# Mixture-of-experts step: experts scattered in pairs, the first overflow job begun in the last turn of the loop

## The chip, the cores and the metric

The kernel runs on one core of one Trainium2 chip. The metric is the device time of one execution in microseconds (us), less is better. The engines are named as in the profile: PE is TensorE, PEld its weight loads, DVE VectorE, ACT ScalarE, POOL GpSimd, SP SyncE, which issues the weight loads from HBM.

## What is computed

One decoder layer in float32 on 320 tokens (256 of a prompt, 64 of samples), width 1024: a convolution and latent-attention mixer, attention into a memory, a layer of 32 experts of which each token takes four, and a final norm. The change touches the experts alone:

```
top_val, top_idx = top_k(h @ w_router + b_router, 4);  gates = softmax(top_val)
for each expert e and its tokens:
    g = min(x @ w_gate[e] + b_gate[e], 7);  u = clip(x @ w_up[e] + b_up[e], -7, 7)
    a = (u + 1) * (g * sigmoid(1.702 * g))
    y[token] += gate * (a @ w_down[e] + b_down[e])
```

Three matrices of 1024 x 1024 float32 belong to an expert, 12.58 MB, and all 32 experts are computed.

## The kernel before

The weights stream through `ring`, four slots of one matrix each, in halves of 2.1 MB: eight halves stand in it, six are used in a turn. SP issues the load of a half as soon as the product that used its place has ended (`refill`, L980), so a half is asked for eight halves ahead of its use, and every load of the expert loop and of the job behind it goes through this one queue in order.

An expert takes at most 64 tokens (`CAP`). The tokens beyond that go to overflow jobs, each of which is one more pass with the same expert's weights; the list `jobs` is computed on the chip. With the inputs here there is one job. Its loads follow those of the loop on SP at once.

A turn of the loop (L830 and on, eight rounds of four turns, so written that `q` is the expert's number modulo 4) runs on PE in this hand-written order:

- `biases` (L809), then the gate product (16 matmuls: two halves of the weights, four chunks, two halves of the output columns, of 64 stationary columns each) into bank 0;
- `scatter(0, ...)`: two matmuls (L822) that put the products of the expert before back onto the tokens 0 to 127, once for each half of the output columns. The stationary operand has 64 rows (the places of one expert) and 128 columns (tokens), so two of them lie in the array side by side in row halves. Results go to banks 6 and 7;
- the up product into bank 1;
- `gather` (L791): six matmuls that select the tokens of the next expert with a one-hot matrix `Ph`;
- `scatter(1, ...)`, tokens 128 to 255;
- `turn_gates` (three transposes of `Pg`, the one-hot matrix times gate), `turn(4, AA)` and `turn(3, XG)` (four transposes each, L319), then `scatter(2, ...)`, tokens 256 to 319;
- the down product into bank 2.

Beside it DVE makes the one-hots of the next expert (`one_hots_at`, L1660 to L1662), clips and multiplies (L1691 to L1702), adds each scattered half into `X` (`add_scattered`, L1674, six additions a turn) and moves the transposed tiles (L1706, L1666). ACT takes the sigmoid (L1254) and copies bank 2 to `XG` (L1257), bank 5 to `PgT` (L1260) and the down product to `Y` (L1263), where the lower 64 rows hold one half of the output columns and the upper 64 the other. `Y` and `PgT` have two buffers.

After the last turn PE scatters the last expert; DVE adds, raises `moe_idle`, and all engines read the number of jobs. Within a job the order is serial: DVE reads the expert's number, shifts the ranks and builds the one-hots (L1721, L1660), PE gathers (L791), turns the gates, ACT copies, PE turns the tokens, DVE moves them, then biases, gate, up, turn, down, scatter into banks 6/7, 0/1 and 3/4, and three wide additions (L1743). The final norm and the stores follow (L1280, L1753, L912).

## Time and profile before

| | us |
|---|---|
| median of three runs (1534.43, 1537.01, 1538.79) | 1537.01 |
| the profiled execution | 1537.16 |
| its span in the profile | 1535.3 |
| one turn of the expert loop | 29.64 |
| last down product of the loop ends | 1471.7 |
| down product of the job ends | 1520.4 |

The first 520 us are the mixer, the memory attention and the router. The expert loop runs from about 520 to 1472 us; the job and the final norm take the rest. The span is the time from the first to the last instruction shown; the execution's own time is 1.9 us longer. A time of an instruction is that of one profiled execution.

### The profile page before, as it was taken

To read this page: it belongs to the slowest core of one execution; us is meant where nothing else is said; L and a number is where in the kernel's file an instruction comes from. 1 tells how busy PE (TensorE), PEld (TensorE's weight loads), DVE (VectorE), ACT (ScalarE), POOL (GpSimd) and SP (SyncE) were. 2 spreads that over 40 slices of the span, in tenths; PEclk is the share of its full clock that TensorE was granted. 3 is DMA by queue.
4 is the path that set the end of the run, shared out by engine and by line. 5 is a ranking of instruction groups with operands and counts; after the bars stand their busy time and mean duration, and the time that the engine had idled before them with its cause. 6 is when DMAs were issued, how large, how long until landed. Compare 5 with 4: busy or idle time off the path is not lost.

```text
span 1535.3 us, 16367 instructions
## 1 busy us (share of the span) xinstructions
PE 1392.9 (91%) x6359; PEld 562.2 (37%) x6359; DVE 520.3 (34%) x1244; ACT 201.2 (13%) x409; POOL 15.9 (1%) x20
## 2 busy tenths in 40 slices
PE   7998667688775899999999999999999999999986
PEld 3574444344534233333333333333333333333322
DVE  1137976312324333223233233323323333232332
ACT  2123212301212000100100100010010010010001
POOL 0100011000000000000000000000000000000000
PEclk9999588899996799999999999999999999999978
DMA  9501011364044299999999999999999999999931
GB/s 341 206 10 36 1 62 62 141 244 194 0 168 175 101 405 422 426 426 423 423 422 429 422 426 426 423 425 425 426 422 426 426 420 426 426 423 421 426 130 35
DMA packets 44235, 463.40 MB, mean 302 GB/s; under 512 B 5174, under 2 KB 6134, under 8 KB 17828
## 3 DMA queue, kind: packets, MB, share of 16 engines
q1 hardware_dynamic: 42668, 453.54, 71.1%
q0 software_dynamic: 1536, 9.44, 1.7%
q8 instruction: 20, 0.33, 0.1%
q14 instruction: 11, 0.09, 0.0%
HBM read 460.04 MB, written 3.28 MB: 302 GB/s over the span
## 4 chain that ended last, share of the span: by engine, by line
PE 87%; DVE 7%; issue 3%; ACT 2%; DMA 1%; POOL 0%; DVEq 0%; SPq 0%; POOLq 0%; ACTq 0%
PE psum L816 45%; PE psum L319 7%; PE psum L822 7%; PE psum L791 6%; PE psum L633 3%; PE psum L387 2%; PE psum L809 2%; DVE ring L1401 2%; PE psum L354 2%; PE psum L372 2%; PE psum L743 1%; PE psum L645 1%; PE psum L540 1%; PE psum L424 1%; DMA ring<-in_w_mk 1%
## 5 line engine op out<-in xcount | busy, mean ns | idle before, releaser
L816 PE MATMUL psum<-ring,work 128*64 128x512 f32 x3168 | 704.1, 597 | 0.8 <-DVE work L1739 0.8
L816 PEld LDWEIGHTS psum<-ring,work 128*64 128x64 f32 x3168 | 219.4, 137 | 477.0 <-issue 456.6
L1674 DVE TENSOR_TENSOR X<-X,psum 128x512 f32<-128x512 f32 (+1 forms) x198 | 126.9, 680 | 107.9 <-PE psum L822 107.9
L1691 DVE TENSOR_SCALAR work<-psum 128x512 f32<-128x512 f32 x32 | 22.2, 692 | 371.7 <-PE psum L816 371.7
L822 PE MATMUL psum<-work 64*128 64x512 f32 (+1 forms) x408 | 116.2, 639 | 2.2 <-DVE X L1674 0.8
L319 PE MATMUL psum<-C,ring 128*128 128x128 f32 (+4 forms) x372 | 59.5, 321 | 58.0 <-DVE ring L1453 22.9
L791 PE MATMUL psum<-H,work 128*64 128x512 f32 (+1 forms) x408 | 101.7, 617 | 7.4 <-DVE work L1662 7.4
L319 PE MATMUL psum<-C,work 128*128 128x128 f32 (+5 forms) x422 | 69.3, 294 | 11.5 <-DMA work<-in_small_rows 6.7
L319 PEld LDWEIGHTS psum<-C,ring 128*128 128x128 f32 (+4 forms) x372 | 50.1, 157 | 70.5 <-DVE ring L1453 27.2
L1699 DVE TENSOR_SCALAR work<-psum 128x512 f32<-128x512 f32 x32 | 22.1, 692 | 150.8 <-PE psum L816 150.8
L1401 DVE SCALAR_TENSOR_TENSOR ring<-ring,cwT 128x256 f32<-128x256 f32 x240 | 72.6, 374 | 0.0
L319 PEld LDWEIGHTS psum<-C,work 128*128 128x128 f32 (+5 forms) x422 | 51.9, 182 | 49.2 <-issue 33.4
L1257 ACT COPY work<-psum 128x512 f32<-128x512 f32 x32 | 18.8, 586 | 302.8 <-PE psum L791 302.8
L791 PEld LDWEIGHTS psum<-H,work 128*64 128x64 f32 (+1 forms) x408 | 26.7, 139 | 78.5 <-issue 71.8
L1254 ACT ACTIVATE work<-work 128x512 f32<-128x512 f32 x32 | 20.2, 630 | 253.1 <-DVE work L1691 253.1
L822 PEld LDWEIGHTS psum<-work 64*128 64x128 f32 (+1 forms) x408 | 28.0, 168 | 64.3 <-issue 55.3
L1263 ACT COPY work<-psum 128x512 f32<-128x512 f32 x32 | 18.8, 586 | 210.1 <-PE psum L816 210.1
L1088 ACT COPY ring<-psum 128x512 f32<-128x512 f32 (+8 forms) x78 | 31.3, 459 | 85.7 <-PE psum L319 81.1
L633 PE MATMUL psum<-ring,work 128*128 128x512 f32 (+1 forms) x96 | 41.6, 593 | 0.7 <-DVE work L1510 0.7
L809 PE MATMUL psum<-work 32*64 32x512 f32 x264 | 36.6, 623 | 1.6 <-DVE work L1666 1.6
L319 PE MATMUL psum<-C,H 128*128 128x128 f32 (+4 forms) x124 | 20.2, 310 | 19.3 <-DVE H L1321 13.3
L387 PE MATMUL psum<-work,ring 128*128 128x320 f32 x128 | 34.6, 432 | 0.0
(249 smaller groups left out, 881.3 us busy)
## 6 DMA issues: line engine op xcount, KB each, us to landing
ring<-in_w_gate SPq DMA_DIRECT2D x66, 2048.0 KB, 9.7
ring<-in_w_up SPq DMA_DIRECT2D x66, 2048.0 KB, 11.5
ring<-in_w_down SPq DMA_DIRECT2D x66, 2048.0 KB, 13.3
ring<-in_w_in SPq DMA_DIRECT2D x1, 4096.0 KB, 28.1
ring<-in_w_out SPq DMA_DIRECT2D x1, 4096.0 KB, 16.0
ring<-in_cache_mem_k SPq DMA_DIRECT2D x8, 512.0 KB, 10.7
ring<-in_cache_mem_v SPq DMA_DIRECT2D x8, 512.0 KB, 13.3
ring<-in_w_in SPq DMA_DIRECT2D x1, 2688.0 KB, 22.8
```

What stands on the lines that cost most here:

```text
L319: return tr(out, in_, C[0:rows, C_ID:C_ID + rows])
L354: last = mm(ps, mT[:, k, 128 * tt:128 * tt + 128], w[:, k, :], start=k == 0, stop=k == KD - 1)
L372: last = mm(ps[0:r, 0:n], hT[:, k, tok(tt)], w_in[:, k, c0:c0 + n], start=k == 0, stop=k == KD - 1)
L387: last = mm(ps[:, 0:T], w_in[:, k, c0 + 128 * m:c0 + 128 * m + 128], hT[:, k, :], start=k == 0, stop=k == KD - 1)
L633: last = mm(ps[0:ROWS[tt], :], mixT[:, k, tok(tt)], w_out[:, k, 512 * nh:512 * nh + 512], start=k == 0, stop=k == KD - 1)
L791: last = mm(psum[64 * nh:64 * nh + 64, 2, :], Ph[0:ROWS[tt], tt, :], xn[0:ROWS[tt], tt, 512 * nh:512 * nh + 512], start=tt == 0, stop=tt == 2)
L809: mm(psum[64 * nh:64 * nh + 64, part, :], sel[q % 2][32 * part:32 * part + 32, :], bgu[32 * part:32 * part + 32, 512 * nh:512 * nh + 512], ...
L816: last = mm(psum[64 * nh:64 * nh + 64, bank, :], src[:, j, 64 * half:64 * half + 64], w[:, half, j, 512 * nh:512 * nh + 512], start=first ...
L822: return mm(psum[0:ROWS[tt], bank + nh, :], PgT[q % 2][64 * nh:64 * nh + 64, tok(tt)], Y[q % 2][64 * nh:64 * nh + 64, :], start=True, stop ...
L1088: last = nc.scalar.copy(dst, src)
L1401: n_ = st(v.scalar_tensor_tensor(acc, u, col, acc, ALU.mult, ALU.add))
L1674: v.tensor_tensor(x, x, psum[0:ROWS[tt], 6 + nh, :], ALU.add).then_inc(s.sc_free, 1)
```

## The change

In the loop the scatter works on pairs of experts. `Pg` holds two experts side by side (64 columns each), so that one set of three transposes per pair gives `PgT` with 128 rows, and `Y` of a pair is kept in two tiles, one for each half of the output columns, with expert 2p in the rows 0 to 63 and expert 2p+1 in 64 to 127. One scatter matmul then has 128 rows and 128 columns. A pair takes five pieces: tokens 0 to 127 and 128 to 255 for each half of the output columns, and a fifth for the 64 tokens that are left, with its two column halves side by side in the array. Three of them are put into the next even turn and two into the next odd one, at the places of the former scatters; the place between the gate and up products of an odd turn is empty. The additions on DVE follow (the fifth piece has two). ACT copies `Y` in two instructions of 64 rows. Banks 6 and 7 alternate by piece.

The data of the first job (ranks, gates, selection of biases) are written to column 32 of `routing` and `C` ahead of the loop, so that the last turn, which builds the one-hots of expert "32", gathers and turns the tokens of the job. After the loop DVE makes the job's gates, the five pieces of the last pair are scattered, and the job begins with its biases and gate product; its gates are turned between gate and up products. Each job gathers the tokens of the one behind it between its up and down products; for the last job that is a gather of tokens that nobody uses. `moe_idle` is gone.

```diff
-        Y = [flat(work, 5120 + 512 * i, 512) for i in range(2)]
+        Y = [[flat(work, 5120 + 512 * i, 512) for i in range(2)],
+             [flat(work, 2048, 512), ckvT[:, :, :].rearrange("p a b -> p (a b)")[:, 0:512]]]
...
-                          Y[q % 2][64 * nh:64 * nh + 64, :], start=True, stop=True)
-
-            def scatter(tt, q, base):
-
-                for nh in range(2):
-                    pe.wait_ge(s.sc_free, base + 2 * tt + nh + 1)
-                    if tt == 2:
-                        pe.sem_inc(s.settled, 1)
-                    scatter_one(tt, nh, q).then_inc(s.sc_full, 1)
+                          Y[q % 2][0][64 * nh:64 * nh + 64, :], start=True, stop=True)
+
+            def scatter_pair(piece, pair, base):
+
+                bank = 6 + (5 * pair + piece) % 2
+                pe.wait_ge(s.sc_free, base + piece + 1)
+                pe.sem_inc(s.settled, 1)
+                if piece < 4:
+                    tt, nh = piece // 2, piece % 2
+                    last = mm(psum[:, bank, :], PgT[pair % 2][:, tok(tt)], Y[pair % 2][nh][:, :],
+                              start=True, stop=True)
+                else:
+                    for nh in range(2):
+                        last = mm(psum[64 * nh:64 * nh + 64, bank, :], PgT[pair % 2][:, tok(2)],
+                                  Y[pair % 2][nh][:, :], start=True, stop=True)
+                last.then_inc(s.sc_full, 1)
...
-            turn_gates(s.pgt_full)
...
-                    e = i * 4 + q
+                    e, pairs = i * 4 + q, i * 2 + q // 2
...
-                            pe.wait_ge(s.pgt_moved, e + 1)
-                            scatter(0, q + 1, e * 6)
+                            pe.wait_ge(s.pgt_moved, pairs + 1)
+                            if q % 2 == 0:
+                                scatter_pair(0, q // 2 + 1, pairs * 5)
...
-                    scatter(1, q + 1, e * 6)
-                    pe.wait_ge(s.pgt_moved, e + 2)
-                    turn_gates(s.pgt_full)
+                    scatter_pair(1 + 2 * (q % 2), q // 2 + 1, pairs * 5)
+                    if q % 2 == 0:
+                        turn_gates(s.pgt_full)
...
-                    scatter(2, q + 1, e * 6)
+                    scatter_pair(2 + 2 * (q % 2), q // 2 + 1, pairs * 5)
...
-            pe.wait_ge(s.pgt_moved, NE + 2)
-            for tt in range(3):
-                scatter(tt, NE + 1, 6 * NE)
-
-
-            pe.wait_ge(s.moe_idle, 1)
+            pe.wait_ge(s.pgt_moved, NE // 2 + 1)
+            for piece in range(5):
+                scatter_pair(piece, NE // 2 + 1, 5 * (NE // 2))
+
+
             further = pe.value_load(jobs[0:1, 0:1], min_val=0, max_val=JOBS)
             with pe.If(further > 0):
                 with pe.Fori(1, further + 1) as n:
+                    pe.wait_ge(s.ov_done, n)
+                    pe.wait_ge(s.ov_xtm, n)
                     pe.wait_ge(s.ov_p, n)
+                    biases(0)
+                    for half in range(2):
+                        pe.wait_ge(ring_in[0][half], (n + USES) * 16)
+                        product(0, XT[0], 0, half, False, half == 1).then_inc(ring_used[0][half], 1)
+                    turn_gates(s.ov_pt)
+                    for half in range(2):
+                        pe.wait_ge(ring_in[1][half], (n + USES) * 16)
+                        product(1, XT[0], 1, half, False, half == 1).then_inc(ring_used[1][half], 1)
+                    pe.wait_ge(s.ov_p, n + 1)
                     gather(s.ov_xg)
-                    turn_gates(s.ov_pt)
+                    pe.wait_ge(s.ov_a, n)
+                    turn(4, AA, s.ov_at)
                     pe.wait_ge(s.ov_xgm, n)
                     turn(3, XG, s.ov_xt)
-                    pe.wait_ge(s.ov_xtm, n)
-                    biases(0)
-                    for t in range(2):
...
-                    pe.wait_ge(s.ov_a, n)
-                    turn(4, AA, s.ov_at)
...
+                    pe.wait_ge(s.sc_free, 5 * (NE // 2) + 7)
                     for tt, bank in enumerate(OV_BANKS):
+                        if tt == 2:
+                            pe.wait_ge(s.ov_xtm, n + 1)
...
-            nc.scalar.memzero(Y[1]).then_inc(s.y_moved, 1)
+            nc.scalar.memzero(Y[1][0])
+            nc.scalar.memzero(Y[1][1]).then_inc(s.y_moved, 1)
             nc.scalar.memzero(PgT[1]).then_inc(s.pgt_moved, 1)
             act.wait_ge(s.xg_full, 1)
             nc.scalar.copy(XG, psum[:, 2, :]).then_inc(s.xg_moved, 1)
-            act.wait_ge(s.pgt_full, 1)
-            nc.scalar.copy(PgT[0], psum[:, 5, 0:T]).then_inc(s.pgt_moved, 1)
...
-                    act.wait_ge(s.pgt_full, e + 2)
-                    act.wait_ge(s.sc_full, e * 6 + 6)
-                    nc.scalar.copy(PgT[(q + 1) % 2], psum[:, 5, 0:T]).then_inc(s.pgt_moved, 1)
+                    if q % 2 == 0:
+                        act.wait_ge(s.pgt_full, i * 2 + (q // 2 + 1))
+                        nc.scalar.copy(PgT[q // 2], psum[:, 5, 0:T]).then_inc(s.pgt_moved, 1)
...
-                    nc.scalar.copy(Y[q % 2], psum[:, 2, :]).then_inc(s.y_moved, 1)
-            act.wait_ge(s.moe_idle, 1)
+                    lo = 64 * (q % 2)
+                    nc.scalar.copy(Y[q // 2][0][lo:lo + 64, :], psum[0:64, 2, :])
+                    nc.scalar.copy(Y[q // 2][1][lo:lo + 64, :], psum[64:128, 2, :]).then_inc(s.y_moved, 1)
+            act.wait_ge(s.rank_done, 1)
             further = act.value_load(jobs[0:1, 0:1], min_val=0, max_val=JOBS)
             with act.If(further > 0):
                 with act.Fori(1, further + 1) as n:
+                    act.wait_ge(s.ov_gc, n)
+                    f(sgm, gm, ACT.Sigmoid, scale=ALPHA).then_inc(s.ov_sg, 1)
+                    act.wait_ge(s.ov_pt, n)
+                    nc.scalar.copy(PgT[0], psum[:, 5, 0:T]).then_inc(s.ov_ptm, 1)
...
-                    v.tensor_scalar(Pg[0:r, tt, :], C[0:r, C_IOTA:C_IOTA + 128], rank, gate, ALU.is_equal, ALU.mult)
+                    v.tensor_scalar(Pg[0:r, tt, lo:lo + 64], C[0:r, C_IOTA:C_IOTA + 64], rank, gate, ALU.is_equal, ALU.mult)
...
+
+            def take_job(n):
+
+                e = dve.value_load(jobs[0:1, bass.ds(n, 1)], min_val=0, max_val=NE - 1)
+                for tt in range(3):
+                    r = ROWS[tt]
+                    v.tensor_scalar(routing[0:r, tt, 2, NE:NE + 1], routing[0:r, tt, 2, bass.ds(e, 1)],
+                                    lists[0:r, bass.ds(n + NE, 1)], None, ALU.subtract)
+                    v.tensor_copy(routing[0:r, tt, 1, NE:NE + 1], routing[0:r, tt, 1, bass.ds(e, 1)])
+                v.tensor_copy(C[0:64, C_SEL + NE:C_SEL + NE + 1], C[0:64, bass.ds(e + C_SEL, 1)]).then_inc(s.ov_rank, 1)
+
+            def job_gates(done):
+
+                for tt in range(3):
+                    r = ROWS[tt]
+                    last = v.tensor_scalar(Pg[0:r, tt, :], C[0:r, C_IOTA:C_IOTA + 128], routing[0:r, tt, 2, NE:NE + 1],
+                                           routing[0:r, tt, 1, NE:NE + 1], ALU.is_equal, ALU.mult)
+                last.then_inc(done, 1)
...
-            def add_scattered(tt, base):
-
-                for nh in range(2):
-                    x = X[0:ROWS[tt], tt, 512 * nh:512 * nh + 512]
-                    dve.wait_ge(s.sc_full, base + (2 * tt + nh + 1))
-                    v.tensor_tensor(x, x, psum[0:ROWS[tt], 6 + nh, :], ALU.add).then_inc(s.sc_free, 1)
+            def add_scattered(piece, pair, base):
+
+                bank = 6 + (5 * pair + piece) % 2
+                dve.wait_ge(s.sc_full, base + piece + 1)
+                if piece < 4:
+                    tt, nh = piece // 2, piece % 2
+                    x = X[:, tt, 512 * nh:512 * nh + 512]
+                    v.tensor_tensor(x, x, psum[:, bank, :], ALU.add).then_inc(s.sc_free, 1)
+                else:
+                    x = X[0:64, 2, 0:512]
+                    v.tensor_tensor(x, x, psum[0:64, bank, :], ALU.add)
+                    x = X[0:64, 2, 512:1024]
+                    v.tensor_tensor(x, x, psum[64:128, bank, :], ALU.add).then_inc(s.sc_free, 1)
...
+            first = dve.value_load(jobs[0:1, 1:2], min_val=0, max_val=NE - 1)
...
+            dve.wait_ge(s.ov_rank, 1)
...
-                    dve.wait_ge(s.sc_free, e * 6 + 2)
-                    add_scattered(0, e * 6)
+                    dve.wait_ge(s.sc_free, pairs * 5 + (2 + 3 * (q % 2)))
+                    if q % 2 == 0:
+                        add_scattered(0, q // 2 + 1, pairs * 5)
...
-            dve.wait_ge(s.sc_free, 6 * NE + 2)
-            for tt in range(3):
-                add_scattered(tt, 6 * NE)
-            dve.wait_ge(s.sc_free, 6 * NE + 8)
-            dve.sem_inc(s.moe_idle, 1)
+            dve.wait_ge(s.pgt_full, NE // 2)
+            job_gates(s.ov_p)
+            dve.wait_ge(s.xt_moved, NE + 1)
+            dve.wait_ge(s.g_clip, NE + 1)
+            dve.wait_ge(s.u_clip, NE + 1)
+            dve.sem_inc(s.ov_xtm, 1)
+            last = 5 * (NE // 2)
+            dve.wait_ge(s.sc_free, last + 2)
+            for piece in range(5):
+                add_scattered(piece, NE // 2 + 1, last)
+            dve.wait_ge(s.sc_free, last + 7)
             further = dve.value_load(jobs[0:1, 0:1], min_val=0, max_val=JOBS)
             with dve.If(further > 0):
                 with dve.Fori(1, further + 1) as n:
-                    e = dve.value_load(jobs[0:1, bass.ds(n, 1)], min_val=0, max_val=NE - 1)
+                    take_job(n + 1)
+                    dve.wait_ge(ring_used[0][1], n + USES)
+                    v.tensor_scalar(gm, psum[:, 0, :], LIMIT, None, ALU.min).then_inc(s.ov_gc, 1)
+                    dve.wait_ge(s.ov_rank, n + 1)
+                    dve.wait_ge(s.ov_pt, n)
                     for tt in range(3):
                         r = ROWS[tt]
-                        v.tensor_scalar(shifted[0:r, tt:tt + 1], routing[0:r, tt, 2, bass.ds(e, 1)],
-                                        lists[0:r, bass.ds(n + NE, 1)], None, ALU.subtract).then_inc(s.ov_rank, 1)
-                    dve.wait_ge(s.ov_rank, n * 3)
-                    dve.sem_inc(s.settled_v, 1)
-                    one_hots_at(e, 0, s.ov_p, shifted)
-                    dve.wait_ge(s.ov_xt, n)
-                    move_tokens(0).then_inc(s.ov_xtm, 1)
-                    dve.wait_ge(ring_used[0][1], n + USES)
-                    v.tensor_scalar(gm, psum[:, 0, :], LIMIT, None, ALU.min).then_inc(s.ov_gc, 1)
+                        v.tensor_scalar(Ph[0:r, tt, :], C[0:r, C_IOTA:C_IOTA + 64], routing[0:r, tt, 2, NE:NE + 1], None,
+                                        ALU.is_equal)
+                    v.tensor_scalar(sel[0][0:64, :], C[0:64, C_ONE:C_ONE + 64], C[0:64, C_SEL + NE:C_SEL + NE + 1], None, ALU.mult)
+                    job_gates(s.ov_p)
...
+                    dve.wait_ge(s.ov_xt, n)
+                    move_tokens(0).then_inc(s.ov_xtm, 1)
```

## Rows read from the trace of the kernel before

**Rows 1.** The page: span; chain by engine; DMA busy in tenths, 40 slices.

```profile
span 1535.3 us, 16367 instructions
...
PE 87%; DVE 7%; issue 3%; ACT 2%; DMA 1%; POOL 0%; DVEq 0%; SPq 0%; POOLq 0%; ACTq 0%
...
DMA  9501011364044299999999999999999999999931
```

**Rows 2.** Windows: busy us per engine (instructions), granted clock, DMA share, GB/s.

```profile
613.06:642.71 29.65, 29.65 (x142) 9.78 (x143) 9.21 (x19) 2.60 (x5) 0.00 (x0) 1.00 1.00 424
...
1471.73:1484.85 13.12, 6.56 (x13) 1.61 (x12) 6.00 (x16) 0.59 (x1) 0.00 (x0) 0.63 0.01 2
1484.85:1493.57 8.72, 7.82 (x28) 2.17 (x28) 0.69 (x1) 0.98 (x2) 0.00 (x0) 0.70 0.00 1
1493.57:1510.20 16.63, 16.61 (x68) 5.08 (x64) 1.39 (x2) 0.63 (x1) 0.00 (x0) 0.84 0.00 0
```

**Rows 3.** Chain of work, one turn of the expert loop: start, us, what.

```profile
612.04 1.02 PE psum L809 x8
613.06 7.02 PE psum L816 x32
620.08 1.06 PE psum L822 x4
...
628.16 2.72 PE psum L791 x12
630.88 1.06 PE psum L822 x4
631.94 1.73 PE psum L319 x11
633.66 1.01 PE psum L822 x4
```

**Rows 4.** Four single weight loads (L980), first and last start, time to landing.

```profile
L980 SPq DMA_DIRECT2D ring<-in_w_up x1: 333/333/333, 883.7 to 883.7; - x1
...
DMA to landing us min/median/max: 11.1/11.1/11.1
...
L980 SPq DMA_DIRECT2D ring<-in_w_down x1: 333/333/333, 895.0 to 895.0; - x1
...
DMA to landing us min/median/max: 14.5/14.5/14.5
...
L980 SPq DMA_DIRECT2D ring<-in_w_up x1: 327/327/327, 1420.5 to 1420.5; - x1
...
DMA to landing us min/median/max: 13.1/13.1/13.1
...
L980 SPq DMA_DIRECT2D ring<-in_w_down x1: 333/333/333, 1458.2 to 1458.2; - x1
...
DMA to landing us min/median/max: 14.6/14.6/14.6
```

**Rows 5.** PE groups by shape, 100 to 520 us: full-array product.

```profile
L633 PE MATMUL psum<-ring,work 128*128 128x512 f32 x64 | 27.7, 593 | 0.7 <-DVE work L1510 0.7
```

**Rows 6.** Chain of work after the expert loop, 1471 us to the end.

```profile
1471.78 0.59 ACT work L1263
...
1474.39 5.44 PE psum L822 x8
...
1480.67 0.55 DVEq L1715
...
1484.85 4.82 PE psum L791 x12
...
1491.86 1.77 PE psum L809 x8
1493.64 16.57 PE psum L816 x64
...
1513.30 7.11 PE psum L816 x32
```

29 lines of the change are left out of this document (15 added, 14 removed).

## Prediction

> **What bounds the kernel now.** I read the page first. The span is 1535.3 us and the chain that ended last is PE for 87% of it, while the DMA tenths stand at 9 from slice 14 to slice 37 [rows 1]. Two resources are thus full in the same stretch, and the whole question is which of them the change relieves. The windows say how full: in one turn of the loop, 29.65 us long, PE is busy for 29.65 us at the full granted clock, and DMA has a share of 1.00 at 424 GB/s [rows 2]. The reader is to see there that both are at their end, and that the PE time of a turn cannot fall without the weights falling behind.
>
> The chain of one turn splits PE's time [rows 3]: biases 1.02, a product 7.02 (three of them), gather 2.72, three scatters 1.06 + 1.06 + 1.01, eleven transposes 1.73. Sum 1.02 + 21.06 + 2.72 + 3.13 + 1.73 = 29.66 us. No wait for DMA stands in it, so PE sets the pace today.
>
> The single loads say what DMA can do [rows 4]. The load issued at 883.7 lands after 11.1, at 894.8; the one issued at 895.0, three loads later, lands after 14.5, at 909.5. Three landings in 14.7 us: one half of a matrix every 4.9 us, although SP had asked for all of them well before. Six are 29.4 us. Now and then one comes a microsecond late, and this makes the mean of a turn about 29.5 to 29.6. DMA is 0.1 to 0.25 us a turn quicker than PE, no more. But there is a store of time: eight halves stand in the ring. The up half issued at 1420.5 (the second half of the last expert) lands after 13.1, at 1433.6 [rows 4], and PE takes it up only at about 1454.6 (the last up product runs in the 7 us before 1458.2). Every half lands some 21 us or more before its use.
>
> After the loop come 13.12 us in which PE is busy for 6.56 and the clock is 0.63, then 8.72 us at 0.70 and 16.63 us at 0.84 [rows 2]. The job is a chain without cover: Y copy, scatter paced by DVE, reading the jobs, one-hots, gather, transposes, tokens moved, biases. From the end of the loop (1471.7) to the start of the job's down product (1513.3) there are 41.6 us [rows 6].
>
> **The loop on PE.** A pair of turns has six scatters today, 2 x 3.13 = 6.26 us. It will have five pieces. Full-array products of the same size, 128 x 128 by 512, took 27.7 us for 64 instructions, two to a product: 0.87 us each [rows 5]. The former scatter at 1.06 us holds 0.87 and about 0.19 for the change of the array's layout. So a piece costs between 0.87 (next to transposes, which have the same layout) and 1.06; I take 0.97, five make 4.85. The fifth piece has the layout of the products and lies next to one. Gates: three of eleven transposes go in every second turn, 3/11 of 1.73 = 0.47. In odd turns nothing lies between gate and up products, 0 to 0.2 saved, 0.1 taken. Sum per pair 6.26 - 4.85 + 0.47 + 0.10 = 1.98 us, 32 us over 16 pairs; the bounds are 6.26 - 5.30 + 0.47 = 1.43 (23 us) and 6.26 - 4.35 + 0.67 = 2.58 (41 us).
>
> What is beside: DVE has 9.21 us of work in a turn of 29.65 and ACT 2.60 [rows 2]. The second Y copy (one more of 0.59 [rows 6]) lies under the biases and the gate product, the additions have a whole product as cover, and the work for the first job ahead of the loop (seven tiny operations and a read of a register, 3 us at most) is due only at the first gather, two products later. I cost these at nothing; if the cover were gone the copy would cost 32 x 0.6 = 19 us. SP issues the same loads in the same order.
>
> **The loop with DMA.** PE shortens a turn by about 1 us, so it takes 28.6 us where the loads take 29.4 to 29.6. The halves then land ever closer to their use; the margin of 21 us is gone after some 22 to 25 turns, and from there on PE waits for the up halves, about 1 us a turn. What sets the end is the landing of the last expert's second up half, at 1433.6 today. It moves forward by what DMA is idle or started late before: the first refill comes 0.5 us earlier (transposes gone ahead of the loop), and the small gaps of the first turns close. I take 1.0 us, estimated between 0.5 and 2. From 1432.6 follow half a product, 3.5, then gather 2.72, a piece 0.97, eight transposes 1.26, the fifth piece 0.9, and the down product 7.02. That is 16.4 us: the loop ends at 1449.0 instead of 1471.7, 22.7 us earlier. It is the same for any PE saving above about 23 us, which even the lower bound gives: of the 32 us some 9 end as waits.
>
> The Trainium skill bears on this in "DMA: Bandwidth & Descriptors", section "Where 436 GB/s comes from". It gives 435 GB/s as the ceiling of the fabric and about 358 as what the HBM side lets a core have, and says that the HBM side binds such loads. By 358 the loop would already be slower than it is; the 424 of [rows 2] is beyond it, so this case's trace disagrees. By 435 a turn's loads would take 28.9 us, an estimate from that page, and the loop would be bound by PE's saving; the landings 4.9 us apart [rows 4] speak for 428.
>
> **From the loop to the job's down product.** After the change, step by step: two Y copies 2 x 0.59 and their signals, 1.3; five pieces 4.9 (banks alternate, and an addition of 0.7 fits under the next piece); reading the number of jobs and branching, which took DVE 0.55 and some steps more up to 1481.8 [rows 6], 1.1; biases 1.0; gate product 7.0; three transposes of gates with the change of layout 0.6; up product 7.0; gather of the next job 2.8, wasted; transposes 1.3 and the move of AT that PE must now await, 0.3. Sum 27.3 us against 41.6. The job's loads are no bound: they land from about 1447 to 1471.8 (the last at 1458.2 + 14.6 = 1472.8 today [rows 4], less 1.0), and PE wants the last at about 1480. The down product starts at 1449.0 + 27.3 = 1476.3 and ends at 1483.4. Behind it nothing is changed: 1535.3 - 1520.4 = 14.9 us. The span would be 1498.3 us at full clock.
>
> **The clock.** It fell to the lower level (1.2 GHz) in the pause behind the loop, where PE was idle for half of 13.12 us [rows 2], first during the Y copy and an addition. At that level the scatters took 5.44 us for eight instructions, the gather 4.82 instead of 2.72, the biases 1.77 instead of 1.02, and the gate and up products 16.57 instead of 14.04 [rows 3, 6]. These last three alone are 5.4 us. The change leaves two pauses, 1.3 us before and 1.1 us behind the five pieces, and the waits for loads of about 1 us in the last turns. The bounds are 0 and 8 us; I take 2.2, nearer to 0 because the 5 us pause of today [rows 2] has gone. The Trainium skill, "TensorE: Matmul & The Clock Gate", section "What's actually happening", says that the throttled level is the default and that activity releases it; by this rule the two short pauses could cost what today's cost, and the result would be about 1508.
>
> **Sum.** 1498.3 + 2.2 = 1500.5 us of span, and 1537.16 - 1535.3 = 1.9 us around it: 1502.4. The profiled execution of before agrees with the median of the three runs to 0.15 us, so this needs no correction. I say 1502 us, 35 us or 2.3% less: 22.7 from the loop, 14.3 from the job less 2.2 for clock.
>
> **The rivals.**
> *DMA is not at its end.* Its 424 GB/s would be PE's pace, and it would go faster when asked. Then the whole PE saving shows: 1471.7 - 32 - 0.5 = 1439, 10 us earlier, 1492 us. Against it stand landings 4.9 us apart with loads queued [rows 4]. Chance 6%.
> *The scatters save nothing.* If changes of layout cost more between a full-array piece and its neighbours (1.25 a piece), only the gates are left, 16 x 0.47 = 7.5 us, and 1537 - 7.5 - 12 = 1517. Against it: 0.87 in [rows 5] and 1.06 in [rows 3]. Chance 8%.
> *The pause stays.* The job might wait for something else, DVE's read of the job or its moves, or the clock might stay low through it, 6 to 8 us more than I sum: 1509. For it: DVE began to read the job at 1480.67 and PE had work again at 1484.85 [rows 6]; against it, PE asks for nothing from that code before the gather. Chance 8%, inside the range.
> *Slower: a piece costs double.* The stationary operand of a piece has 128 rows by 128 columns of float32, where two former scatters share the array. If that form ran at half the rate beside the strided PSUM use here, a piece would be 1.71: 5 x 1.71 - 6.26 - 0.47 = 1.8 us more per pair, 29 us, less the 13 us of the job, 1553 us. It decides from 1.5 us a piece on, where the loss in the loop equals the 13 us. Only [rows 5] speaks against it, but strongly. Chance 3%.
>
> **How the numbers follow.** The forecast has 75%, DMA free 6%, scatters worth nothing 8%, pause stays 8%, slower 3%. The range 1492 to 1514 takes in the DMA rival's centre, the clock's 8 us, late loads of 2 us and unseen waits of 3 us, and leaves out the scatter rival and the slow one. What a measurement can tell from no change is about 0.3%, 4.6 us. Faster by more holds 95%; the tails of the scatter rival and of the slow one give 2% for no difference and 3% for slower.
>
> **What would show it.** Right: turns of about 28.6 us at first; time to landing growing from turn to turn to some 30 us and more; PE waits on ring loads only from about the 23rd turn, ahead of up products; the loop's last product ending near 1449; the last weight load landing near 1472 as before; the first job product some 8 us after the loop's last. Wrong: landings closer than 4.85 us (DMA rival); pieces above 1.1 us; waits on DVE between the pieces; the lower clock level beyond the first part of the job.

## The result

The changed kernel takes 1497.59 us (median of four runs, 1495.99 to 1499.05); the kernel before took 1537.79 in the same comparison. The ratio is 0.9742 (95% interval 0.9723 to 0.9761), and a second comparison gave 0.9744 (0.9728 to 0.9759). That is 40 us or 2.6% less, where 1502 was forecast. One execution of the run `job_only` below was in a slower state (1577.97 us, at a granted clock of 0.90 where the others have 0.94 or 0.95) and is left out of its median.

The page of the changed kernel, to be set beside [rows 1]:

```profile
span 1496.0 us, 15598 instructions
...
PEclk9999687889998599999999999999999999999998
DMA  9601002346107069999999999999999999999993
...
PE 76%; DMA 13%; DVE 6%; issue 3%; ACT 2%; POOL 0%; SPq 0%; POOLq 0%; ACTq 0%; DVEq 0%
```

DMA now stands in the chain with 13%, where it had 1%, and PE has fallen from 87% to 76%. The clock row keeps its 9s to the end of the loop and through the job; the tenths of DMA in the loop are unchanged, because they were at 9 already.

Two consecutive turns of the loop, early, in the chain of work (start, us, what), the counterpart of [rows 3]:

```profile
614.49 1.02 PE psum L810 x8
615.50 13.88 PE psum L817 x64
629.39 2.72 PE psum L792 x12
632.11 1.05 PE psum L833 x2
633.17 0.95 PE psum L320 x8
634.12 1.01 PE psum L837 x4
635.12 6.87 PE psum L817 x32
...
650.03 1.06 PE psum L833 x2
...
660.82 1.05 PE psum L833 x2
661.88 1.58 PE psum L320 x11
663.46 0.86 PE psum L833 x2
```

The five pieces of a pair stand at 1.05, 0.86, 1.06, 1.05 and 1.01 us. The gate and up products of the odd turn run as one block of 13.88 in place of 14.04, and the transposes take 1.58 (eleven) and 0.95 (eight) in place of 1.73 twice. A pair of turns that nothing holds takes 56.85 us (from the biases at 641.99 to those at 698.84) where it took 59.28.

Late in the loop the chain (same columns) looks different: once in two turns it runs through a load.

```profile
1313.45 3.65 PE psum L817 x16
...
1330.73 7.04 PE psum L817 x32
...
1337.79 34.47 DMA ring<-in_w_up
...
1372.30 3.65 PE psum L817 x16
```

The load that PE waits for was asked for 34.5 us earlier. The time to landing has grown on the way, as the forecast had it. For the up halves of the whole loop it is, first in the kernel before, then in the changed one:

```profile
DMA to landing us min/median/max: 9.2/11.5/13.5
```

```profile
DMA to landing us min/median/max: 7.8/26.3/34.5
```

In the kernel before it stays where it is from the first turn to the last, with one to three halves under way whenever one lands; in the changed kernel it climbs turn by turn, until six or seven are under way. One single load, the second up half of the last expert, as in [rows 4]:

```profile
L994 SPq DMA_DIRECT2D ring<-in_w_up x1: 328/328/328, 1396.6 to 1396.6; - x1
...
DMA to landing us min/median/max: 34.5/34.5/34.5
```

It was issued at 1396.6 and lands at 1431.1; in the kernel before the same half landed at 1433.6 [rows 4]. PE stood ready for it, as the forecast had it. Windows (busy us and instructions per engine, granted clock, DMA share, GB/s) of one late pair, of the stretch from the loop's end to the job's first product, and from there to its down product, to compare with [rows 2]:

```profile
1334.35:1393.20 58.85, 57.29 (x265) 19.07 (x263) 14.77 (x32) 5.17 (x9) 0.00 (x0) 1.00 1.01 428
1447.40:1455.13 7.73, 6.01 (x21) 1.81 (x21) 4.00 (x6) 1.16 (x2) 0.00 (x0) 1.00 0.99 421
1455.13:1473.99 18.86, 18.82 (x91) 6.63 (x88) 5.88 (x20) 1.64 (x3) 0.00 (x0) 1.00 0.71 301
```

A late pair takes 58.85 us, PE is busy for 57.29 of it, and DMA moves 428 GB/s: that is twelve halves, one in 4.904 us. Behind the loop the clock is 1.00 throughout, where [rows 2] had 0.63, 0.70 and 0.84. The chain there (start, us, what), against [rows 6]:

```profile
1440.52 6.89 PE psum L817 x32
...
1448.06 0.55 ACT ckvT L1278
...
1448.75 1.96 PE psum L833 x4
...
1454.11 1.09 PE psum L810 x8
...
1462.21 0.57 PE psum L320 x3
...
1469.81 2.72 PE psum L792 x12
...
1473.99 7.11 PE psum L817 x32
```

The loop ends at 1447.4 (before: 1471.7). The second Y copy ends at 1448.6, five pieces follow to 1453.8, the job's biases start at 1454.1, its products follow with one block of transposes between, and the down product starts at 1473.99, 26.6 us behind the end of the loop in place of 41.6.

Where the 39.3 us of the span are: up to the first gather the changed kernel was 2.0 us later (518.47 against 516.49), which is no more than single executions scatter (the traces of the changed kernel and its variants have that gather between 513.6 and 518.5, those with the loop of before between 513.7 and 516.5); from there to the first product of the loop 0.9 us was lost; the loop from its first product to its end took 920.4 in place of 947.7, 27.3 less; the stretch to the job's down product 15.0 less; the rest is equal, 22.0. 27.3 + 15.0 - 2.0 - 0.9 = 39.4.

### The profile page after: what moved, and what is told of

It is laid out like the page before. It is cut to its first block, busy times and chain, and to the rows that moved or that the text cites. A ratio compares the mean times of both kernels' runs of the same rounds, so it can differ in the third digit from the quotient of the medians.

```text
span 1496.0 us, 15598 instructions
## 1 busy us (share of the span) xinstructions
PE 1352.7 (90%) x6116; PEld 556.6 (37%) x6116; DVE 464.1 (31%) x1162; ACT 212.8 (14%) x425; POOL 15.8 (1%) x20
## 4 chain that ended last, share of the span: by engine, by line
PE 76%; DMA 13%; DVE 6%; issue 3%; ACT 2%; POOL 0%; SPq 0%; POOLq 0%; ACTq 0%; DVEq 0%
PE psum L817 38%; DMA ring<-in_w_up 11%; PE psum L320 6%; PE psum L792 5%; PE psum L833 4%; PE psum L634 3%; PE psum L388 2%; DVE ring L1416 2%; PE psum L355 2%; PE psum L810 2%; PE psum L373 2%; PE psum L744 1%; PE psum L646 1%; PE psum L837 1%; PE psum L541 1%
## 5 line engine op out<-in xcount | busy, mean ns | idle before, releaser
L1710 DVE TENSOR_TENSOR X<-X,psum 128x512 f32<-128x512 f32 x68 | 46.7, 686 | 90.0 <-PE psum L833 89.9
L320 PE MATMUL psum<-C,work 128*128 128x128 f32 (+5 forms) x371 | 56.8, 287 | 10.5 <-DMA work<-in_small_rows 6.8
L320 PEld LDWEIGHTS psum<-C,work 128*128 128x128 f32 (+5 forms) x371 | 48.7, 187 | 35.9 <-issue 22.3
L1270 ACT COPY work<-psum 128x512 f32<-128x512 f32 x32 | 18.8, 586 | 292.9 <-PE psum L792 292.9
L1277 ACT COPY work<-psum 64x512 f32<-64x512 f32 x32 | 18.5, 578 | 286.6 <-PE psum L817 286.6
L833 PE MATMUL psum<-work 128*128 128x512 f32 x100 | 54.6, 628 | 1.4 <-ACT ckvT L1278 1.4
L634 PE MATMUL psum<-ring,work 128*128 128x512 f32 (+1 forms) x96 | 41.6, 593 | 0.7 <-DVE work L1525 0.7
L810 PE MATMUL psum<-work 32*64 32x512 f32 x264 | 36.8, 627 | 1.1 <-DVE work L1700 0.8
L355 PE MATMUL psum<-ring 128*128 128x512 f32 x64 | 30.7, 644 | 2.7 <-DMA ring<-in_w_mk 2.7
```

The source lines that it names most:

```text
L320: return tr(out, in_, C[0:rows, C_ID:C_ID + rows])
L355: last = mm(ps, mT[:, k, 128 * tt:128 * tt + 128], w[:, k, :], start=k == 0, stop=k == KD - 1)
L634: last = mm(ps[0:ROWS[tt], :], mixT[:, k, tok(tt)], w_out[:, k, 512 * nh:512 * nh + 512], start=k == 0, stop=k == KD - 1)
L810: mm(psum[64 * nh:64 * nh + 64, part, :], sel[q % 2][32 * part:32 * part + 32, :], bgu[32 * part:32 * part + 32, 512 * nh:512 * nh + 512], ...
L833: last = mm(psum[:, bank, :], PgT[pair % 2][:, tok(tt)], Y[pair % 2][nh][:, :], start=True, stop=True)
L1710: v.tensor_tensor(x, x, psum[:, bank, :], ALU.add).then_inc(s.sc_free, 1)
```

## The experiments

In all of them I read from the trace the length of the loop, from the start of its first gate product to the end of its last down product, because the start of the loop itself varies by some microseconds from execution to execution of one kernel:

| kernel | loop from, to | length | time, median | ratio to before |
|---|---|---|---|---|
| before | 524.06, 1471.73 | 947.7 | 1537.8 | 1 |
| changed | 526.96, 1447.4 | 920.4 | 1497.6 | 0.9742 |
| pairs_only | 526.81, 1447.28 | 920.5 | 1510.1 | 0.9828 |
| job_only | 522.03, 1469.71 | 947.7 | 1525.5 | 0.9941 |
| after_less | 526.42, 1437.32 | 910.9 | 1487.2 | 0.9674 |
| after_16more | 526.69, 1451.34 | 924.6 | 1501.2 | 0.9772 |
| after_32more | 526.40, 1464.75 | 938.3 | 1515.3 | 0.9851 |
| after_late | 522.09, 1452.09 | 930.0 | 1506.0 | 0.9803 |
| before_late | 521.49, 1469.16 | 947.7 | 1538.2 | 1.0008 |
| before_less | 521.26, 1468.93 | 947.7 | 1537.2 | 1.0005 |
| after_warm | 525.35, 1443.38 | 918.0 | 1492.2 | 0.9708 |
| after_warm_all | 524.66, 1442.72 | 918.1 | 1492.1 | 0.9704 |
| after_trim | 526.56, 1445.85 | 919.3 | 1495.5 | 0.9732 |
| after_again | 524.35, 1444.74 | 920.4 | 1498.2 | 0.9744 |

The theory: in the changed kernel the loads, one unbroken stream, set the end of the loop, and PE waits for them at its end; the job's new order is worth some 14 us of its own. The rivals: PE's own work sets the end of the loop; or the two parts pay only together.

**Each part alone.** `pairs_only` puts the old job code behind the new loop (with `moe_idle`, the one-hots built from the shifted ranks behind the last addition, and the old order in the job). Against the changed kernel:

```diff
-            first = dve.value_load(jobs[0:1, 1:2], min_val=0, max_val=NE - 1)
...
-            job_gates(s.ov_p)
...
+            dve.sem_inc(s.moe_idle, 1)
...
+                    job_one_hots(e)
+                    dve.wait_ge(s.ov_xt, n)
+                    move_tokens(0).then_inc(s.ov_xtm, 1)
```

> The scatter in pairs is kept, the job behind the loop is as in the kernel before (its tokens gathered after the last addition). If the loop's gain is 24.3 us (its end at 1447.4 in place of 1471.7) and independent of the job, the time is 1537 - 24 + 1 for the second Y copy in the pause = 1514 us, and the clock falls in the pause again. If the loop's gain came only together with the new job order, it is above 1520.

`job_only` leaves the loop as before and takes the new preparation and the new job code, on PE, ACT and DVE. Against the kernel before:

```diff
+            first = dve.value_load(jobs[0:1, 1:2], min_val=0, max_val=NE - 1)
...
+            dve.wait_ge(s.pgt_full, NE + 1)
+            job_gates(s.ov_p)
...
-            dve.sem_inc(s.moe_idle, 1)
```

> The loop is as before (six scatters of 64 rows a pair, gates turned in each turn), the job begins as in the changed kernel. Theory: the stretch from the end of the loop to the down product of the job shrinks from 41.6 to about 27 us, 1537 - 14 = 1523 us, and the turn stays at 29.64. Rival, the job order is worth only its busy time saved (some 5 us) and the rest was the clock by chance: about 1532.

Measured: `pairs_only` 1510.06, ratio 0.9828 (0.9811 to 0.9844), 26 us less than the kernel before in that comparison, and a loop of 920.5 us, that of the changed kernel. That is 4 us below the expected 1514, where the second Y copy was to cost 1 us in the pause: from the loop's end to the job's down product this trace has 40.6 us, against 41.6 before. `job_only` 1525.50, ratio 0.9941 (0.9922 to 0.9961), 9 to 10 us less, with the loop of before; expected were 14. The parts stand on their own, and 0.9828 times 0.9941 is 0.9770, close to 0.9742 but above it. The trace of `job_only` shows what is missing (timeline of PE: start, us, engine, line, form, count, idle before):

```profile
1472.36 5.46 PE L822 MATMUL psum<-work 64*128 64x512 f32 x8 [0.84 <-DVE X L1698]
1477.75 1.98 PE L809 MATMUL psum<-work 32*64 32x512 f32 x8
1479.67 8.84 PE L816 MATMUL psum<-ring,work 128*64 128x512 f32 x32
...
1500.29 7.09 PE L816 MATMUL psum<-ring,work 128*64 128x512 f32 x32
```

With the six scatters of the old form, the first two of them between waits of 0.69 us on ACT and 0.84 us on DVE, the clock still falls: from 1469.7 to 1477.8 it is granted at 0.70, under the biases at 0.50. The last four scatters take 5.46 for eight instructions, the biases 1.98, the gate product 8.84. From the loop's end to the job's down product it takes 30.6 us, where the changed kernel takes 26.6 and before took 41.6. So of the 15.0 us the order of the job alone brings 11.0, and 4.0 come with the five pieces, during and behind which the granted clock was 1.00.

**Is it the loads that end the loop?** `after_less` leaves out a quarter of the bytes of each down half in the loop.

```diff
             def load_half(m, half, src):
-                dst = slot(m % 4)[:, half].rearrange("p j n -> p (j n)")
-                dma(dst, src[half]).then_inc(ring_in[m % 4][half], 16)
+                n = 3072 if m >= 4 and m % 3 == 2 else 4096
+                dst = slot(m % 4)[:, half].rearrange("p j n -> p (j n)")[:, 0:n]
+                dma(dst, src[half][:, 0:n]).then_inc(ring_in[m % 4][half], 16)
```

> The changed kernel, but the loads of the down matrices bring three quarters of their bytes (the last chunk of each row stays as it was, so the down products are partly computed with old weights): a turn's loads take 27.0 us in place of 29.4. Theory, the loads set the end of the loop: PE now runs free, a pair takes 56.85 us throughout, the loop ends 14 to 15 us earlier, time about 1483 us. Rival, PE's own work or something else set the end and the waits on loads are incidental: no change, 1497.

Measured 1487.21, ratio 0.9674 (0.9653 to 0.9695), and no wait of PE on a load in the loop. The loop is 910.9 us, 9.5 us shorter than that of the changed kernel. The theory holds; the size, 9.5 and not 14 to 15 us, is what PE really waits. The trace of the changed kernel gives the same sum: from the 23rd turn on, the second up half of each of ten turns starts late, and set beside `after_less`, start against start, these ten delays make 9.5 us. The idle time that the profile shows ahead of them is less, 7.3 us in nine waits (below), because the ends of matmuls in it are modelled. The same edit in the kernel before:

> The kernel before with three quarters of the bytes of the down matrices in the loop and in nothing else (the down products are partly computed with old weights). Theory: PE sets its pace, no change, 1537 us. Rival, traffic of the loads slows PE or binds the loop: 5 us or more less.

Measured 1537.16, ratio 1.0005 (0.9992 to 1.0017), loop 947.7: the kernel before did not depend on the bytes of the loads at all, and PE does not run faster for having less traffic beside it, so that the 9.5 us of `after_less` are waits.

**How much PE work is free now?** A scatter done twice, with the same result, in odd turns (`piece == 3`) or in every turn (`piece in (1, 3)`):

```diff
-                    last = mm(psum[:, bank, :], PgT[pair % 2][:, tok(tt)], Y[pair % 2][nh][:, :],
-                              start=True, stop=True)
+                    for _ in range(2 if base is not last_base and piece == 3 else 1):
+                        last = mm(psum[:, bank, :], PgT[pair % 2][:, tok(tt)], Y[pair % 2][nh][:, :],
+                                  start=True, stop=True)
```

> The changed kernel with the first scatter of each odd turn done twice (same result), 16 matmuls of 0.87 us, 14 us more work for PE in the loop. Theory, the loads set the end and PE waits for them some 14 us in all: time unchanged within 1 us, 1498 us. Rival, PE sets the pace: 1511 us.

> The changed kernel with one scatter of each turn done twice, 32 matmuls of 0.87 us, 28 us more for PE, twice as much as the waits on loads that the changed kernel has. Theory, loads as the bound with 14 to 15 us of waits to be used up: 13 us more than the changed kernel, 1511 us, and a turn at PE's pace with hardly a wait. Rival, PE sets the pace: 28 us more, 1525.

Measured: `after_16more` 1501.16, ratio 0.9772 (0.9756 to 0.9789), `after_32more` 1515.29, ratio 0.9851 (0.9827 to 0.9876). Neither expectation is met (1498 and 1511), and neither is the rival (1511 and 1525): 14 us of work cost 4, 28 us cost 18. With the 910.9 us of `after_less` as PE's own time both fall into place: 910.9 + 13.9 = 924.8 against 924.6 measured, and 910.9 + 27.8 = 938.7 against 938.3. The loop takes the larger of PE's own time and 920.4. The free part is 9.5 us, not the 14 that I had put down.

**Is it a stream whose start counts?** SP asks for each half one matrix later:

```diff
                 for half in range(2):
-                    sp.wait_ge(ring_used[m % 4][half], i * 3 + m // 4)
+                    sp.wait_ge(ring_used[(m + 1) % 4][half], i * 3 + (m + 1) // 4)
```

> The changed kernel, but SP asks for each half of the loop one matrix later (six halves ahead in place of eight). Nothing else is touched. Theory, the loads are one unbroken stream whose start sets the end of the loop: the stream starts 8 us later, so the time is 8 us more, 1505 to 1506 us. Rival, the ring's depth does not matter: no change.

> The kernel before with the same late requests. Theory: its loads land 21 us or more ahead of their use, one matrix less leaves 10 us or more, no change: 1537 us. Rival, the kernel before is bound by its loads too: about 8 us more.

Measured: `after_late` 1505.96, ratio 0.9803 (0.9780 to 0.9826), 8.4 us above the changed kernel; `before_late` 1538.19, ratio 1.0008 (0.9997 to 1.0019). The waits of PE on loads in the loop (total, times, longest), first in the changed kernel, then in `after_late`:

```profile
PE psum L817 <- DMA ring<-in_w_up: 7.3, 9, 1.1
```

```profile
PE psum L817 <- DMA ring<-in_w_up: 14.9, 19, 1.1
```

With less of the ring as store PE meets the loads earlier, in 19 turns in place of 9, and everything shifts by the late start: counted from the first gather, the first refill is asked for 8.1 us later than in the changed kernel (22.7 against 14.7) and the loop ends 9.6 us later; the other 1.5 us lie in the stream itself, 891.7 us from first landing to the last expert's second up half in place of 890.2. The kernel before is given the same late start and does not feel it.

**The clock at the start of the loop.** The traces showed something that the prediction lacks. Timeline of the changed kernel (start, us, engine, line, form, count, idle before):

```profile
525.05 1.98 PE L810 MATMUL psum<-work 32*64 32x512 f32 x8 [0.79 <-DVE work L1700]
...
526.96 9.37 PE L817 MATMUL psum<-ring,work 128*64 128x512 f32 x32
...
533.13 3.77 SPq L994 DMA_DIRECT2D ring<-in_w_up  x2
```

The same place in the kernel before:

```profile
523.04 1.09 PE L809 MATMUL psum<-work 32*64 32x512 f32 x8 [0.79 <-DVE work L1666]
524.06 7.09 PE L816 MATMUL psum<-ring,work 128*64 128x512 f32 x32
527.94 3.77 SPq L980 DMA_DIRECT2D ring<-in_w_up  x2
```

The biases take 1.98 in place of 1.09 and the first gate product 9.37 in place of 7.09. In both kernels the clock is at its lower level (1.2 GHz, granted 0.50) when the gather starts and rises during it. In the kernel before it stays up. In the changed kernel the three transposes of gates that stood ahead of the loop are gone, PE is idle for 0.69 and 0.79 us around the four that are left, and the clock falls again, to 1.2 GHz, from about 525 to 532. The second of these pauses is there in the kernel before too; the first is what the removed transposes filled. From the first gather to the first refill 14.7 us pass (518.47 to 533.13) in place of 11.5 (516.49 to 527.94), so the stream of loads starts 3.2 us late, and since it sets the end of the loop, that is lost in full. `after_warm` fills the two gaps with five transposes each of constants, into a bank nobody reads:

```diff
             gather(s.xg_full)
+            for _ in range(5):
+                flip(psum[:, 5, 0:128], C[:, C_ONE:C_ONE + 128], P)
             pe.wait_ge(s.xg_moved, 1)
             turn(3, XG, s.xt_full)
+            for _ in range(5):
+                flip(psum[:, 5, 0:128], C[:, C_ONE:C_ONE + 128], P)
```

> The changed kernel with four-column-block transposes of constants nobody reads ahead of the loop: five behind the first gather and five behind the first turn of the tokens, where the three transposes of gates have gone and the clock fell in the changed kernel (biases 1.98 and first product 9.37 us at the lower level, against 1.09 and 7.09 before). Theory: the clock stays up, the first refill comes 3 us earlier after the first gather, and since the loads are one unbroken stream the whole gain shows: 1494.5 us against 1497.6. Rival: the loop ends where it did because PE's start is not what holds the loads, no change.

```profile
524.33 1.09 PE L810 MATMUL psum<-work 32*64 32x512 f32 x8 [0.24 <-DVE work L1704]
...
525.35 7.09 PE L817 MATMUL psum<-ring,work 128*64 128x512 f32 x32
...
529.23 3.77 SPq L998 DMA_DIRECT2D ring<-in_w_up  x2
```

Measured 1492.18 (1490.08 to 1494.80, five runs), ratio 0.9708 (0.9686 to 0.9730). The clock stays up, the first refill comes 11.5 us after the first gather (517.73 to 529.23), and from the first gather to the end of the loop it takes 925.7 us in place of 928.9: 3.2 us, as worked out. The medians differ by 5.4 us, of which I can explain 3.2; the rest is of the size by which single executions differ up to the first gather. The changed kernel was run once more to see whether the difference is luck:

> The changed kernel once more, unchanged, for an interval to set beside that of after_warm (0.9708, 0.9686 to 0.9730). If the cold start of the loop is a loss of 3 us, the ratio to the kernel before is 0.973 to 0.974 again; if after_warm was a lucky draw, it is 0.971.

Measured 1498.20, ratio 0.9744 (0.9728 to 0.9759): the two intervals overlap by 0.0002. All five executions of `after_warm` (1490.08 to 1494.80) are shorter than all nine of the changed kernel (from 1495.30 on), so that it beats the changed one too, by 0.4% going by the medians, at the edge of what times alone can show, and by 3.2 us or 0.2% going by the traces.

**More of the same.** `after_warm_all` adds 13 products of constants in PE's idle places from 488 us on (seven ahead of the ranks, two and one between them, three behind the down biases), and four transposes in each of the two gaps.

```diff
+            def filler(n):
+                for _ in range(n):
+                    mm(psum[:, 5, :], C[:, C_ONE:C_ONE + 128], C[:, 0:512], start=True, stop=True)
+
+            filler(7)
             pe.wait_ge(s.routed, 3)
...
+            filler(3)
             emptied(pe, V, ("bd", 2, 1))
```

> As the run above, and idle places of PE ahead of the loop (the router's ranks, the biases of the down products) filled with 13 products of constants, so that the clock is at its upper level from there on. Theory: the six down-bias products fall from 10.8 to about 6 us, the first gather from 4.4 to 2.7, ranks by 1.5, the loop's start by 3; the stream of loads starts 10 to 11 us earlier and the time is about 1487 us. Rival, the clock does not rise in these gaps or the filling delays the real work: 1494 or more.

Measured 1492.14, ratio 0.9704 (0.9684 to 0.9724), the same as `after_warm`. Windows before and behind the start of the down biases:

```profile
494.00:503.00 9.00, 7.69 (x35) 4.10 (x33) 4.83 (x26) 0.00 (x0) 0.00 (x0) 1.00 0.00 0
503.00:518.50 15.50, 14.97 (x20) 4.69 (x20) 6.00 (x14) 0.00 (x0) 0.00 (x0) 0.56 0.08 34
```

The down biases and the filling products behind them in the timeline of PE:

```profile
503.53 9.82 PE L789 MATMUL psum<-keep 32*128 32x512 f32 x12 [0.89 <-DVE keep L1673]
513.28 5.27 PE L760 MATMUL psum<-C 128*128 128x512 f32 x6
```

The clock rose and held 1.00 until the ranks were done, then fell to the lower level again among the down biases, which took 9.82 us (before 10.79), and the three filling products cost 5.3 us at that level. The expectation of 1487 us failed. What came of the filling stands in the first gather, 2.9 us in place of 4.4, and in the start of the loop; the time is that of `after_warm`. It was no pause that held the clock down here: behind the 0.89 us ahead of the first down bias PE was busy without a break, 14.97 of the 15.50 us. The down biases use 32 of the 128 rows of the array and the filling products all of them, and the clock was low under both. What lowered it these runs do not show.

**The gather that nobody uses.** `after_trim` leaves out, within a job, the gather and the move of the next job's tokens, and with them DVE's reading of the next job and its one-hots.

```diff
-                    pe.wait_ge(s.ov_p, n + 1)
-                    gather(s.ov_xg)
                     pe.wait_ge(s.ov_a, n)
                     turn(4, AA, s.ov_at)
-                    pe.wait_ge(s.ov_xgm, n)
-                    turn(3, XG, s.ov_xt)
```

> The changed kernel without the gather, copy, turn and move of the tokens of the next job inside a job (which is right only where there is one job, as here): 3.5 us less of PE's work on the path behind the loop, of which about 1.6 us come back as the wait for the activation that they covered. Theory: 1.5 to 2 us less, 1495.7 us, at the edge of what can be measured; the profile's stretch from the up product's end to the down product's start falls from 4.2 to about 2.4 us.

Measured 1495.52, ratio 0.9732 (0.9712 to 0.9752), not to be told from 0.9742. Timeline of PE:

```profile
1469.86 0.75 PE L320 MATMUL psum<-C,work 128*128 128x128 f32 x4 [1.59 <-DVE work L1776]
1471.38 8.59 PE L817 MATMUL psum<-ring,work 128*64 128x512 f32 x32 [0.78 <-DVE work L1778]
```

The stretch from the up product's end to the down product's start fell by 1.0 us, from 4.2 to 3.2, but PE was idle for 1.59 and 0.78 us in it, the clock fell, and the down product took 8.59 in place of 7.09. In this trace the useless gather cost nothing, because without it the clock fell. Whether such pauses always have that price is not shown: in the kernel before PE was idle for the same 1.59 and 0.78 us at this place, the clock stayed up, and the down product took 7.11 [rows 6]. Nor is the loss at the start of the loop the same in every execution. Ahead of the loop `after_trim` is the changed kernel, yet its first gate product took 8.26 us, where seven other traces with this start have 9.37 or 9.38.

## Why the prediction held, and where it was off

**The bound.** That PE alone set the pace before, and that the loads would take over, is shown from both sides: `before_less` and `before_late` change nothing, `after_less` and `after_late` move the changed kernel by -9.5 (its loop) and +8.4 us. The signs that I had named came too: turns of 28.4 us at first, waits ahead of up products from the 23rd turn on, 34.5 us from issue to landing, the end of the loop at 1447.4, the last landing at 1470.3, the first product of the job 7.8 us behind the loop.

**PE's saving in the loop.** Forecast 1.98 us a pair, measured 59.28 - 56.85 = 2.43. The pieces cost 5.03 where I took 4.85, so that term was a little too small. The gates were mis-sized more: I took 3/11 of the block, 0.47 us, but the two blocks of transposes went from 3.46 to 2.53, 0.93 less. Eleven transposes next to full-array pieces took 1.58 in place of 1.73, so about 0.15 a block comes, as I read it, from a change of layout saved; I did not test that apart. The products of a pair gave 0.31 (13.88 and 6.87 in place of 14.04 and 7.02) where I took 0.10. It made no difference to the time, as forecast: what exceeds some 27 us goes into waits.

**The landing that sets the end.** Forecast 1432.6, measured 1431.1. Two errors nearly cancelled here, so that it came so close is luck. I let the stream start 0.5 us earlier; measured from the first gather it started 3.2 us later, since I had counted the three removed transposes as a gain of 0.5 and not as the work that held the clock. Against that, the stream from its first landing to this one took 890.2 us (540.9 to 1431.1) in place of 896.5 (537.1 to 1433.6), 181 intervals of 4.92 in place of 4.95 us, where I had counted on some 0.5 us from small gaps that close.

The 6.3 us come from a term that I had misread. I took the 29.5 to 29.6 us a turn, and the late landings in it, for a property of the loads. But the kernel before asks for a half only when PE has freed its place, twelve in 59.28 us or one in 4.94, and its time to landing does not grow (9.2 to 13.5 us all through the loop). So its loads kept up with PE and came at PE's pace, and their landings did not tell how fast loads can be. With more asked for ahead they came 4.904 us apart. 181 intervals would be 894.1 us at the one pace and 887.6 at the other; both streams are 2.4 to 2.6 us longer. The window of [rows 2] could not show it: the DMA share was 1.00 there at 424 GB/s, and it was 1.00 again when the loads set the pace, at 428.

The late landings cost little beside that. In the kernel before, twelve intervals were longer than 5.15 us (up to 6.3), in the changed kernel four, the last ending at 622 us. In the longest of the kernel before (a window as in [rows 2]) the DMA engines worked on:

```profile
701.01:707.33 6.32, 6.32 (x34) 2.02 (x36) 0.00 (x0) 0.59 (x1) 0.00 (x0) 1.00 0.98 412
```

Why they come at all the runs do not show.

**The waits.** Forecast some 9 us, measured 9.5 by `after_less`. That the two agree is luck as well, since both sides of the difference were off by the same: PE's saving was 36.8 us in the loop (947.7 to 910.9) and not 32, and 27.3 of it showed and not 22.7. While planning the experiments I put 14 there, by taking 24.3 us, the difference of the two ends of the loop, from 38.9 (16 pairs at 2.43), and forgetting the 3.2 us lost at its start and the 2.0 us by which this execution began later.

**From the loop to the job's down product.** Forecast 27.3, measured 26.6: two Y copies 1.4 (1.3), five pieces 5.1 (4.9), reading the number of jobs 0.3 (1.1; the reading is not on PE's path for as long as DVE's row suggested), then 19.9 (20.0).

**The clock.** I took 2.2 us behind the loop and none ahead of it. It was the other way round: nothing behind, 3.2 us ahead, of which 2.3 in the first product. The rule of the Trainium skill that I had cited ("TensorE: Matmul & The Clock Gate", "What's actually happening": the throttled level is the default, activity releases it) bears on a place that I did not look at, the 2.2 us between the end of the first gather and the loop; by this rule less activity there can let the clock fall, and the trace agrees, 9.37 us for the first product against 7.09, and 7.09 again with the filling of `after_warm`. The trace of `after_warm_all` does not agree at another place, the down biases, where PE was busy for 14.97 of 15.50 us and the mean clock was 0.56; there the measurement decides.

**Sum.** The span was 1496.0 where 1500.5 was forecast: 1.6 from the end of the loop, 0.7 from the stretch to the job's down product, 2.2 from the clock. Of the rivals, the free DMA is ruled out by `after_less` and `after_16more`, and by the 4.904 us between landings that did not shrink with six or seven loads waiting: it gave 428 GB/s in place of 424 and no more. The worthless scatters and the doubled piece are ruled out by the rows of the turn, and the pause that stays by the chain behind the loop.

## What to carry to other kernels

Where PE is full and DMA is full beside it, the busy shares do not say which of them sets the pace (DMA stood at 1.00 in both kernels). Ask whether the time from issue to landing grows, and how far ahead of its use each load lands. A ring that is always full is a store of time, and a saving on PE is worth at most that store plus what the stream itself gains. From then on what counts is when the stream starts, and a microsecond ahead of the first refill is worth a whole one. Before removing small work from PE ahead of a long run of products, look at the granted clock on both sides of it: idle gaps of 0.7 us beside few matmuls cost more there than the work removed, and cheap filling work gave it back. Look at the clock again behind any filling: ahead of the down biases it bought nothing, the clock fell although PE was busy.

## What the runs showed of the hardware

- A full-array float32 product of 512 columns costs 0.86 us beside transposes of the same layout and 1.05 beside column-split ones, and eleven transposes gain as well, 1.58 in place of 1.73: a change of layout is worth, as an estimate from these rows, 0.15 to 0.2 us.
- The loads of 2.1 MB landed 4.904 us apart (428 GB/s) for 58.85 us of a pair, with six or seven of them under way and with PE at 97%; 34.5 us from issue to landing did not slow them. With one to three under way they followed PE's pace, 4.94 us.
- PE's clock fell at the start of the loop after idle gaps of 0.69 and 0.79 us and did not fall behind the loop after 1.36 us of idle time that followed 7 us of products and was followed by five pieces with gaps of 0.1 us at most. It fell ahead of the job's down product after 1.59 and 0.78 us in `after_trim` and not after the same pauses in the kernel before, and it fell in `after_warm_all` under products that followed each other without a pause. What decides these runs don't show.
